# Two norms in a row computed from one residual, with the first one's rescale of the residual moved behind the next projection

## The chip, the cores and the metric

The kernel runs on one NeuronCore of a Trainium2 chip. Time is device time of one execution in microseconds. Five engines work from queues of their own: TensorE (PE) for matrix products, VectorE (DVE) and ScalarE (ACT) for elementwise work, GpSimd (POOL), which is idle around the change, and SyncE (SP), whose queue starts the loads of the weights.

## The reference

Two stacks of two layers each run over 256 tokens of 1024 features, in f32. The first stack ends with a norm of its own (`final_norm`), and the second one begins with a gated FFN that norms its input once more. What the change touches is this:

```python
RMS_EPS = EPS = 1e-6
def rms_norm(x, g):                       # _rms is the same
    x32 = x.astype(jnp.float32)
    y = x32 * lax.rsqrt(jnp.mean(x32 * x32, axis=-1, keepdims=True) + RMS_EPS)
    return (y * g.astype(jnp.float32)).astype(x.dtype)

def _swiglu(h, w_in, w_out):
    gate, up = jnp.split(h @ w_in, 2, axis=-1)
    return (jax.nn.silu(gate) * up) @ w_out

# end of the first stack
x = x + 0.5 * swiglu_ffn(rms_norm(x, ffn2_norm[1]), ffn2_w_in[1], ffn2_w_out[1])
x = rms_norm(x, final_norm)
# begin of the second one
x = x + 0.5 * _swiglu(_rms(x, norm_gain[0, 0]), ffn_w_in[0, 0], ffn_w_out[0, 0])
```

## The kernel before

The residual X lies in SBUF as eight chunks of 128 features by 256 tokens, so features are on the partitions. A product in f32 precision is made of three in the type fp32r: each operand is split into a high part (a copy rounded to fp32r, ScalarE) and a low part (what is left, VectorE), and TensorE adds high x high, low x high and high x low. The activations' parts are `Hh`/`Hl` (or `Ah`/`Al` inside an FFN), the weights' are `hi`/`lo`.

Weights come in slabs through a ring of four: SyncE loads a slab into `raw` (`sp_stage`), ScalarE makes `hi` (`act_hi`, L339), VectorE makes `lo` (`dve_lo`, L347), TensorE multiplies. A slab of the first projection of an FFN (`ffn_in`) has 8 weight tiles, so 24 products; one of the second projection (`ffn_out`) has 11, so 33, and two slabs make one tile of 128 output features. A load waits for the low part of the slab three places earlier; `act_hi` waits for TensorE to be done with the slab four places earlier.

An FFN with number n is the stages `ffn_in`n and `ffn_out`n. In `ffn_in` VectorE and ScalarE scale, gate and split each result (L724 `gate`, L701 Silu, L728 `up`, L732, L705 `Ah`, L736 `Al`). In `ffn_out` VectorE adds each tile to its chunk of X (`dve_resid`, L623), then chunk by chunk `prep` makes what the next norm and projection need: ScalarE makes `Hh`, the chunk times the next gain (L561), and its square (L565), VectorE makes `Hl` (L569) and adds the squares up in `SQSUM` (L576, L579). The factor 1/rms itself is a number per token and so is applied to the result of the projection (`R`, in L724 and L728), not to its input. So the next stage can start while the norm is still being computed: TensorE takes the first pair of slabs up to chunk 6 (`first_pair`, L451 to L453), then does the norm's sum over the partitions, one product of `SQSUM` with a matrix of ones (`norm`, L645), then chunk 7 of the pair, then the loop (L470, L475, L476). ScalarE takes the square root of the sum (L650) and VectorE the reciprocal (L655), which gives `R`.

The blocks run in this order: ffn0, rwkv (with the memory's keys), xattn0, ffn1, ffn2, gmlp, xattn1, ffn3, final, ffn4, hgrn, ffn5, ffn6, dil, ffn7. The block `final` is the class `FinalNorm`. It is set apart from the others by the list `UNSPLIT`: in `ffn_out3` `prep` makes only the squares. Then `FinalNorm` does the norm's product, 13 filler products that nothing reads (`pe_keep_awake`, L406), root and reciprocal, multiplies all eight chunks of X by gain and 1/rms (L1154), and makes `Hh`, `Hl` and the squares of the new X in one go. Each engine works its program in the order in which the blocks stand; there is no scheduler. ScalarE loads the table for the square root at the end of `act_resid` (L610) and that for Silu after the root (L652).

`ffn_out5` is a useful neighbour: there `prep` makes a second split of X for the attention's keys (`keys_hi`, L411, and `keys_lo`, L416), one operation more on each of the two engines in a tile.

## Time and profile before

| | us |
|---|---|
| median of three timed runs | 2582.8 |
| the three runs | 2577.11, 2582.8, 2590.47 |
| span of the profiled execution, first to last instruction | 2575.4 |
| TensorE busy in it | 2501.2 (97%) |
| VectorE busy | 1745.3 (68%) |
| ScalarE busy | 1318.1 (51%) |

The profiler took one execution of its own; its time beyond the span is not in the page. In the timeline views, a row gives the start, the busy time, engine, line, operation, written tile and read tiles, the count of instructions merged, and in brackets the idle time of the engine before it and what ended that. Products are pipelined: each has 0.28 us of its own, but they follow each other every 0.113 us at full clock. A product of full f32 type is two records.

### The profile page before, as it was taken

The page shows a single profiled execution, that of the slowest core. Times are in us where ns is not written, and L with a number is a line of the kernel's source. Part 1 is how long each engine was busy: PE and PEld are TensorE (multiplying, and loading weights), DVE is VectorE, ACT ScalarE, POOL GpSimd, SP SyncE. Part 2 cuts the span into 40 slices and gives each one's busy share as a digit, 9 for nine tenths or more (in the row PEclk, how much of TensorE's full clock was granted, in tenths as well). Part 3 has the DMA queues.
Part 4 walks back from the last instruction along what each step waited for, and adds up shares of the span by engine and source line. Part 5 has one row for each costly group of instructions (what it writes and reads, how often), then busy time and mean ns, then how long its engine had stood idle before and what let it go on. Part 6 is the DMA issues. An engine that isn't in the chain of part 4 may idle for free.

```text
span 2575.4 us, 60687 instructions
## 1 busy us (share of the span) xinstructions
PE 2501.2 (97%) x23366; PEld 2432.5 (94%) x23366; DVE 1745.3 (68%) x2868; ACT 1318.1 (51%) x1998; POOL 79.0 (3%) x122
## 2 busy tenths in 40 slices
PE   8998998999999999999999999899999999999999
PEld 7997877989999999989999999899999999999999
DVE  5757677567757667767757756967667666666774
ACT  5544544455545555545545547455555455555552
POOL 0000442000000000000000000000000000000000
PEclk9999999999999999999999999999999999999999
DMA  5663301435655655445654655235655665553564
GB/s 198 203 215 133 100 11 43 148 125 182 209 184 183 219 200 176 157 138 181 209 174 155 209 174 195 84 115 195 206 173 200 204 177 153 161 160 105 192 211 138
DMA packets 119681, 424.89 MB, mean 165 GB/s; under 512 B 16657, under 2 KB 24420, under 8 KB 119268
## 3 DMA queue, kind: packets, MB, share of 16 engines
q1 hardware_dynamic: 111328, 410.73, 47.6%
q10 hardware_dynamic: 8196, 11.96, 2.4%
q8 instruction: 112, 1.84, 0.3%
q14 instruction: 45, 0.37, 0.0%
HBM read 421.51 MB, written 1.12 MB: 164 GB/s over the span
## 4 chain that ended last, share of the span: by engine, by line
PE 89%; DVE 5%; ACT 3%; issue 2%; POOL 1%; DMA 0%; ACTq 0%; SPq 0%; DVEq 0%; POOLq 0%
PE bank L476 21%; PE bank L470 21%; PE bank L475 21%; PE bank L396 5%; PE bank L398 4%; PE bank L397 4%; PE bank L2327 1%; ACT hi L339 1%; PE bank L451 1%; PE bank L452 1%; PE bank L453 1%; DVE lo L347 1%; PE bank L1730 1%; PE bank L1703 1%; PE bank L1715 1%
## 5 line engine op out<-in xcount | busy, mean ns | idle before, releaser
L347 DVE TENSOR_TENSOR lo<-raw,hi 128x1024 fp32r<-128x1024 f32 (+1 forms) x728 | 935.0, 1292 | 380.6 <-ACT hi L339 378.8
L339 ACT ACTIVATE hi<-raw 128x1024 fp32r<-128x1024 f32 (+1 forms) x728 | 782.6, 1106 | 297.1 <-PE bank L398 170.6
L470 PE MATMUL bank<-Hh,hi 128*128 128x256 f32 x3056 | 845.5, 277 | 4.6 <-DVE lo L347 4.4
L476 PE MATMUL bank<-Hh,lo 128*128 128x256 f32 x3056 | 845.9, 277 | 0.0
L475 PE MATMUL bank<-Hl,hi 128*128 128x256 f32 x3042 | 840.8, 276 | 0.0
L470 PEld LDWEIGHTS bank<-Hh,hi 128*128 128x128 f32 x3056 | 574.5, 188 | 6.2 <-DVE lo L347 5.6
L476 PEld LDWEIGHTS bank<-Hh,lo 128*128 128x128 f32 x3056 | 574.5, 188 | 0.0
L475 PEld LDWEIGHTS bank<-Hl,hi 128*128 128x128 f32 x3042 | 572.2, 188 | 0.0
L476 PE MATMUL bank<-Ah,lo 128*128 128x256 f32 x1408 | 389.3, 277 | 0.0
L470 PE MATMUL bank<-Ah,hi 128*128 128x256 f32 x1408 | 388.6, 276 | 0.0
L475 PE MATMUL bank<-Al,hi 128*128 128x256 f32 x1400 | 386.4, 276 | 0.0
L470 PEld LDWEIGHTS bank<-Ah,hi 128*128 128x128 f32 x1408 | 264.3, 188 | 0.0
L476 PEld LDWEIGHTS bank<-Ah,lo 128*128 128x128 f32 x1408 | 264.3, 188 | 0.0
L475 PEld LDWEIGHTS bank<-Al,hi 128*128 128x128 f32 x1400 | 262.8, 188 | 0.0
L701 ACT ACTIVATE sgate<-gate 128x256 f32<-128x256 f32 x176 | 73.5, 418 | 232.2 <-DVE gate L724 232.2
L705 ACT ACTIVATE Ah<-act 128x256 f32 (+1 forms) x176 | 73.7, 419 | 209.1 <-DVE act L732 209.1
L623 DVE SCALAR_TENSOR_TENSOR X<-bank,X 128x256 f32<-128x256 f32 x112 | 47.4, 424 | 170.8 <-PE bank L476 163.1
L396 PE MATMUL bank<-Hh,hi 128*128 128x256 f32 x528 | 151.9, 288 | 0.0
L561 ACT ACTIVATE Hh<-X,vec 128x256 fp32r<-128x256 f32 x104 | 51.9, 503 | 193.6 <-DVE X L623 190.6
L398 PE MATMUL bank<-Hh,lo 128*128 128x256 f32 x528 | 147.7, 280 | 0.0
L397 PE MATMUL bank<-Hl,hi 128*128 128x256 f32 x528 | 147.7, 280 | 0.0
L396 PE MATMUL bank<-Kh,hi 128*128 128x256 f32 x384 | 112.3, 292 | 0.0
(429 smaller groups left out, 4038.8 us busy)
## 6 DMA issues: line engine op xcount, KB each, us to landing
raw<-in_w SPq DMA_DIRECT2D x600, 512.0 KB, 3.4
raw<-in_w SPq DMA_DIRECT2D x128, 704.0 KB, 4.5
dB<-dil_bias ACTq DMA_DIRECT2D x16, 384.0 KB, 10.4
X<-in_x SPq DMA_DIRECT2D x2, 512.0 KB, 5.3
mem_x<-in_mem ACTq DMA_DIRECT2D x2, 512.0 KB, 3.2
gWS<-in_ws ACTq DMA_DIRECT2D x1, 1024.0 KB
gBS<-in_bs ACTq DMA_DIRECT2D x1, 1024.0 KB
out_x<-X SPq DMA_DIRECT2D x4, 256.0 KB, 2.6
```

The costliest lines, as they stand in the source:

```text
L339: act.activation(k.hi[:, q, :w], k.raw[:, q, :w], ACT.Copy).then_inc(k.hi_ready, 1)
L347: dve.tensor_tensor(k.lo[:, q, :w], k.raw[:, q, :w], k.hi[:, q, :w].bitcast(F32), ALU.subtract).then_inc(k.lo_ready, 1)
L396: pe.matmul(out, wh, xh, start=first and kc == 0, stop=False)
L397: pe.matmul(out, wh, xl, start=False, stop=False)
L398: mm = pe.matmul(out, wl, xh, start=False, stop=last)
L470: pe.matmul(out, wh, xh, start=first, stop=False)
L475: pe.matmul(out, wh, xl, start=False, stop=False)
L476: mm = pe.matmul(out, wl, xh, start=False, stop=last)
L561: eng.activation(k.Hh[:, c, :], src[:, c, :], ACT.Copy, scale=k.v1(gain, c)).then_inc(k.h_hi, 1)
L623: dve.scalar_tensor_tensor(k.X[:, c, :], k.bank[s % RING][:, :T], coef, k.X[:, c, :], ALU.mult, ALU.add).then_inc(k.banks_freed, st.per_tile)
L701: act.activation(k.sgate[:, j, :], k.gate[:, j, :], ACT.Silu).then_inc(k.silu_done, 1)
L705: act.activation(k.Ah[:, bass.ds(m, 1), :].rearrange("p a t -> p (a t)"), k.act32[:, j, :], ACT.Copy).then_inc(k.ah_ready, 1)
```

## The change

With y = x r g, where r = 1/rms(x) and g is `final_norm`, the second norm is y r' g' with r' = 1/rms(y). Its mean of squares is r^2 mean((x g)^2), so r r' = 1/sqrt(mean((x g)^2) + eps mean(x^2) + eps^2). The changed kernel uses that:

- In `ffn_out3` `prep` splits the unscaled X times the product of both gains (`both_gains`, made once at the start of ffn3 on VectorE, 128x8), and adds up two sums: `SQSUM` of x^2 as before, and `FSUM` of (x g)^2 by way of `FSQ`. After the last chunk one fused operation adds eps times `SQSUM` to `FSUM`.
- ffn4 uses `norm_twice` in place of `norm`: two products on the matrix of ones into the halves of bank 4, two square roots (`STD` and `FSTD`), the load of the Silu table, and the reciprocal of the first, which is `R` for ffn4.
- `dve_final_norm` takes the reciprocal of `FSTD` and rescales X. It stands between ffn4's `ffn_in` and its first residual.
- The class `FinalNorm` with its fillers is gone.

```diff
@@ column_masks
-            low * HEAD ** -0.5, (1 - low) * HEAD ** -0.5]
+            low * HEAD ** -0.5, (1 - low) * HEAD ** -0.5, np.full(P, EPS * EPS)]
...
-UNSPLIT = ("final_norm", "mix_norm0")
+UNSPLIT = ("mix_norm0",)
...
@@ prep
-        k = self.k
+        k, twice = self.k, gain == "final_norm"
         ns, nq = self.split_n[e] + c, self.square_n[e] + c
+        scale = k.both_gains[:, c:c + 1] if twice else k.v1(gain, c)
         if e == "act":
...
+            if twice:
+                if c >= 2:
+                    eng.wait_ge(k.fsq_added, c - 1)
+                eng.activation(k.FSQ[:, c % 2, :], src[:, c, :], ACT.Square, scale=k.v1(gain, c)).then_inc(k.fsq_ready, 1)
         else:
...
+            if twice:
+                eng.wait_ge(k.fsq_ready, c + 1)
+                if c == 0:
+                    ins = eng.tensor_copy(k.FSUM[:], k.FSQ[:, 0, :])
+                else:
+                    eng.wait_ge(k.fsq_added, c)
+                    ins = eng.tensor_tensor(k.FSUM[:], k.FSUM[:], k.FSQ[:, c % 2, :], ALU.add)
+                ins.then_inc(k.fsq_added, 1)
+                if c == NC - 1:
+                    eng.wait_ge(k.fsq_added, NC)
+                    eng.wait_ge(k.sq_added, nq + 1)
+                    eng.scalar_tensor_tensor(k.FSUM[:], k.SQSUM[:], EPS, k.FSUM[:], ALU.mult, ALU.add).then_inc(k.fsum_ready, 1)
...
+    def norm_twice(self, eng, e, then=None):
+        k, n = self.k, self.norm_n[e]
+        if e == "pe":
+            self.square_n["pe"] += NC
+            eng.wait_ge(k.sq_added, self.square_n["pe"])
+            eng.wait_ge(k.fsum_ready, 1)
+            eng.matmul(k.bank[4][:, :T], k.ones, k.FSUM[:], start=True, stop=True)
+            eng.matmul(k.bank[4][:, T:], k.ones, k.SQSUM[:], start=True, stop=True).then_inc(k.ss_ready, 1)
+        elif e == "act":
+            eng.wait_ge(k.ss_ready, n + 1)
+            eng.wait_ge(k.rstd_ready, n)
+            eng.activation(k.STD[:], k.bank[4][:, :T], ACT.Sqrt, bias=k.col(C_EPS_SQUARED), scale=1.0 / D).then_inc(k.std_ready, 1)
+            eng.activation(k.FSTD[:], k.bank[4][:, T:], ACT.Sqrt, bias=k.col(C_EPS), scale=1.0 / D).then_inc(k.fstd_ready, 1)
+            eng.preload_act_table(then)
+        else:
+            eng.wait_ge(k.std_ready, n + 1)
+            eng.reciprocal(k.R[:], k.STD[:]).then_inc(k.rstd_ready, 1)
+        self.norm_n[e] += 1
+
+    def dve_final_norm(self, dve):
+        k = self.k
+        dve.wait_ge(k.fstd_ready, 1)
+        dve.reciprocal(k.FSTD[:], k.FSTD[:]).then_inc(k.frstd_ready, 1)
+        dve.wait_ge(k.frstd_ready, 1)
+        for c in range(NC):
+            dve.scalar_tensor_tensor(k.X[:, c, :], k.X[:, c, :], k.v1("final_norm", c), k.FSTD[:],
+                                     ALU.mult, ALU.mult).then_inc(k.x_scaled, 1)
+        dve.wait_ge(k.x_scaled, NC)
...
@@ FeedForward.dve
-        sh.norm(dve, "dve")
+        if self.next_gain == "final_norm":
+            g0, g1 = (k.vec[:, COL[n]:COL[n] + NC] for n in ("final_norm", GAIN_OF["ffn4"]))
+            dve.tensor_tensor(k.both_gains[:], g0, g1, ALU.mult).then_inc(k.both_ready, 1)
+        self.norm(dve, "dve")
...
         run(dve, st, body)
+        if self.normed_twice:
+            sh.dve_final_norm(dve)
         sh.dve_resid(dve, self.st_out, 0.5, self.next_gain, self.keys_next)
...
-class FinalNorm:
...
-    def pe(self, pe):
-        self.sh.norm(pe, "pe")
-        self.sh.pe_keep_awake(pe, 13, self.k.ones)
...
```

Where instructions stand, in the program's order. VectorE from the last residual chunk of `ffn_out3` on, before (L1154 is the rescale, L569 the low part of the activations):

```order
L623 SCALAR_TENSOR_TENSOR X<-bank,X 128x256
L579 TENSOR_TENSOR SQSUM<-SQSUM,SQ 128x256
L347 TENSOR_TENSOR lo<-raw,hi 128x1024 x2
L655 RECIPROCAL R<-STD 128x256
L1154 SCALAR_TENSOR_TENSOR X<-X,vec,R 128x256 x8
L569 SCALAR_TENSOR_TENSOR Hl<-X,vec,Hh 128x256
L576 COPY SQSUM<-SQ 128x256
L569 SCALAR_TENSOR_TENSOR Hl<-X,vec,Hh 128x256
L579 TENSOR_TENSOR SQSUM<-SQSUM,SQ 128x256
```

The same place in the changed program, from the last chunk's split on (L583 is the low part, L593 and L601 the two sums, L606 the fused one, L702 the reciprocal):

```order
L649 SCALAR_TENSOR_TENSOR X<-bank,X 128x256
L583 SCALAR_TENSOR_TENSOR Hl<-X,both_gains,Hh 128x256
L593 TENSOR_TENSOR SQSUM<-SQSUM,SQ 128x256
L601 TENSOR_TENSOR FSUM<-FSUM,FSQ 128x256
L606 SCALAR_TENSOR_TENSOR FSUM<-SQSUM,FSUM 128x256
L354 TENSOR_TENSOR lo<-raw,hi 128x1024 x2
L702 RECIPROCAL R<-STD 128x256
L206 UNCONDITIONAL_BRANCH
L206 ISA
L785 ISA
```

The reciprocal for ffn4 now stands right behind the weights' low parts. The rescale is not there any more; it stands behind the last low part of `ffn_in4` (L798), ahead of the first residual of `ffn_out4` (L649):

```order
L794 TENSOR_TENSOR act_59<-sgate,up 128x256
L354 TENSOR_TENSOR lo<-raw,hi 128x1408
L798 TENSOR_TENSOR Al<-act_59,Ah 128x256
L709 RECIPROCAL FSTD<-FSTD 128x256
L712 SCALAR_TENSOR_TENSOR X<-X,vec,FSTD 128x256 x8
L649 SCALAR_TENSOR_TENSOR X<-bank,X 128x256
L583 SCALAR_TENSOR_TENSOR Hl<-X,vec,Hh 128x256
```

TensorE from the last products of `ffn_out3` into the first pair of `ffn_in4`, before:

```order
L476 MATMUL bank<-Ah,lo 128x256
L518 REGISTER_ALU
L518 COMPARE_AND_BRANCH
L645 MATMUL bank<-SQSUM,masks 128x256
L406 MATMUL bank<-masks 128x256 x13
L451 MATMUL bank<-Hh,hi 128x256
L452 MATMUL bank<-Hl,hi 128x256
```

In the changed program the first pair follows the projection directly (L458 to L460), and the norm's products stand ahead of its chunk 7, two in a row:

```order
L460 MATMUL bank<-Hh,lo 128x256
L692 MATMUL bank<-FSUM,masks 128x256
L693 MATMUL bank<-SQSUM,masks 128x256
L458 MATMUL bank<-Hh,hi 128x256
L459 MATMUL bank<-Hl,hi 128x256
L460 MATMUL bank<-Hh,lo 128x256
```

So the norm's product, the 13 fillers and the second norm's product became two products inside the pair.

## Rows read from the trace of the kernel before

**Rows 1.** The page of the profile: its first line and part 1
```profile
span 2575.4 us, 60687 instructions
...
PE 2501.2 (97%) x23366; PEld 2432.5 (94%) x23366; DVE 1745.3 (68%) x2868; ACT 1318.1 (51%) x1998; POOL 79.0 (3%) x122
```

**Rows 2.** Timeline of TensorE at the final norm: start us, us, operation, count, [idle before]
```profile
1347.65 0.28 PE L476 MATMUL bank<-Ah,lo 128*128 128x256 f32 x1
1349.48 0.70 PE L645 MATMUL bank<-SQSUM,masks 128*128 128x256 f32 x2 [1.55 <-DVE SQSUM L579]
1350.02 5.78 PE L406 MATMUL bank<-masks 128*128 128x256 f32 x26
1358.33 0.55 PE L451 MATMUL bank<-Hh,hi 128*128 128x256 f32 x1 [2.54 <-DVE Hl L569]
...
1366.56 0.28 PE L470 MATMUL bank<-Hh,hi 128*128 128x256 f32 x1
```

**Rows 3.** Timeline of VectorE over the same stretch
```profile
1348.04 0.42 DVE L623 SCALAR_TENSOR_TENSOR X<-bank,X 128x256 f32<-128x256 f32 x1 [3.26 <-PE bank L476]
...
1352.62 1.75 DVE L655 RECIPROCAL R<-STD 128x256 f32<-128x256 f32 x1 [0.37 <-ACT STD L650]
1354.41 3.25 DVE L1154 SCALAR_TENSOR_TENSOR X<-X,vec,R 128x256 f32<-128x256 f32 x8
1357.70 0.48 DVE L569 SCALAR_TENSOR_TENSOR Hl<-X,vec,Hh 128x256 fp32r<-128x256 f32 x1
...
1362.69 0.48 DVE L569 SCALAR_TENSOR_TENSOR Hl<-X,vec,Hh 128x256 fp32r<-128x256 f32 x1
```

**Rows 4.** Stretches there: busy us (x) of PE, PEld, DVE, ACT, POOL; granted clock; DMA
```profile
1358.00:1360.00 2.00, 1.67 (x8) 1.70 (x9) 2.00 (x7) 1.58 (x5) 0.00 (x0) 0.54 0.00 0
1360.00:1362.00 2.00, 2.00 (x11) 1.91 (x11) 2.00 (x7) 2.00 (x6) 0.00 (x0) 0.60 0.00 0
```

**Rows 5.** Timeline of TensorE between the second and third FFN, with no norm between
```profile
771.84 0.28 PE L476 MATMUL bank<-Ah,lo 128*128 128x256 f32 x1
...
776.72 0.59 PE L645 MATMUL bank<-SQSUM,masks 128*128 128x256 f32 x2
776.96 0.47 PE L451 MATMUL bank<-Hh,hi 128*128 128x256 f32 x1
...
777.86 0.28 PE L470 MATMUL bank<-Hh,hi 128*128 128x256 f32 x1
```

**Rows 6.** Timeline of VectorE where the fourth FFN (ffn3) begins
```profile
1173.28 1.75 DVE L655 RECIPROCAL R<-STD 128x256 f32<-128x256 f32 x1 [2.11 <-ACT STD L650]
```

**Rows 7.** Timeline of VectorE in the projection ahead of the keys (ffn_out5)
```profile
1884.50 0.42 DVE L623 SCALAR_TENSOR_TENSOR X<-bank,X 128x256 f32<-128x256 f32 x1 [1.34 <-PE bank L476]
...
1891.98 0.42 DVE L623 SCALAR_TENSOR_TENSOR X<-bank,X 128x256 f32<-128x256 f32 x1 [2.46 <-PE bank L476]
...
1893.79 0.48 DVE L416 SCALAR_TENSOR_TENSOR Kl<-X,vec,Kh 128x256 fp32r<-128x256 f32 x1
```

**Rows 8.** Timeline of ScalarE between the second and third FFN
```profile
777.35 0.47 ACT L650 ACTIVATE STD<-bank,cols 128x256 f32<-128x256 f32 x1 [0.64 <-PE bank L645]
...
780.39 0.42 ACT L701 ACTIVATE sgate<-gate 128x256 f32<-128x256 f32 x1 [1.26 <-DVE gate L724]
```

**Rows 9.** Timeline of VectorE where ffn4's first projection ends and its second begins
```profile
1484.83 1.62 DVE L347 TENSOR_TENSOR lo<-raw,hi 128x1408 fp32r<-128x1408 f32 x1
1486.37 0.42 DVE L736 TENSOR_TENSOR Al<-act,Ah 128x256 fp32r<-128x256 f32 x1
1488.83 0.42 DVE L623 SCALAR_TENSOR_TENSOR X<-bank,X 128x256 f32<-128x256 f32 x1 [2.04 <-PE bank L476]
...
1491.40 3.16 DVE L347 TENSOR_TENSOR lo<-raw,hi 128x1408 fp32r<-128x1408 f32 x2 [0.81 <-ACT hi L339]
```

**Rows 10.** Timeline of TensorE in ffn4's second projection: first product, first on slab 4
```profile
1481.07 0.28 PE L470 MATMUL bank<-Ah,hi 128*128 128x256 f32 x1
...
1496.15 0.28 PE L470 MATMUL bank<-Ah,hi 128*128 128x256 f32 x1
```

More of the change, by code:

```diff
@@ L519, in pe_stage, with pe_first_stage @@
                 body(i)
-    def pe_first_stage(self, pe, st, late=False, pair=False):
+    def pe_first_stage(self, pe, st, late=False, pair=False, norm=None):
         self.split_n["pe"] += NC
-        self.pe_stage_h(pe, st, lambda: self.norm(pe, "pe"), late, pair=pair)
+        self.pe_stage_h(pe, st, lambda: (norm or self.norm)(pe, "pe"), late, pair=pair)
     def pe_stage_h(self, pe, st, after_first=None, late=False, rest=False, pair=False):
@@ L669, with __init__ @@
 class FeedForward:
-    def __init__(self, sh, name, order, nxt, keys_next=False, keys_now=False):
+    def __init__(self, sh, name, order, nxt, keys_next=False, keys_now=False, normed_twice=False):
         self.sh, self.k, self.n, self.next_gain = sh, sh.k, order, nxt
+        self.norm = sh.norm_twice if normed_twice else sh.norm
+        self.normed_twice = normed_twice
         self.keys_next, self.keys_now = keys_next, keys_now
@@ L681, in pe @@
             sh.pe_keep_awake(pe, 5, k.X[:, 0, :P], k.X[:, 1, :])
-        sh.pe_first_stage(pe, self.st_in, late=self.n == 0)
+        sh.pe_first_stage(pe, self.st_in, late=self.n == 0, norm=self.norm)
         done = 2 + FC * self.n
@@ L689, in act @@
         sh, k, st = self.sh, self.k, self.st_in
-        sh.norm(act, "act", ACT.Silu)
+        self.norm(act, "act", ACT.Silu)
         if self.keys_now:
@@ L1131, in dve @@
         sh.dve_resid(dve, self.so, 1.0, self.next_gain)
-class FinalNorm:
-    def __init__(self, sh, name, nxt):
-        self.sh, self.k, self.next_gain = sh, sh.k, nxt
-    def pe(self, pe):
-        self.sh.norm(pe, "pe")
-        self.sh.pe_keep_awake(pe, 13, self.k.ones)
-    def act(self, act):
-        k = self.k
-        self.sh.norm(act, "act")
-        self.sh.prep_all(act, "act", k.X, self.next_gain, wait=lambda c: act.wait_ge(k.x_scaled, c + 1))
-    def dve(self, dve):
-        k = self.k
-        self.sh.norm(dve, "dve")
-        dve.wait_ge(k.rstd_ready, self.sh.norm_n["dve"])
-        for c in range(NC):
-            dve.scalar_tensor_tensor(k.X[:, c, :], k.X[:, c, :], k.v1("final_norm", c), k.R[:],
-                                     ALU.mult, ALU.mult).then_inc(k.x_scaled, 1)
-        dve.wait_ge(k.x_scaled, NC)
-        self.sh.prep_all(dve, "dve", k.X, self.next_gain)
 class Hgrn2:
@@ L3004, in make_blocks @@
         gain = "final_norm" if nxt == "final" else GAIN_OF.get(nxt)
+        if b == "final":
+            continue
         if b.startswith("ffn"):
-            out.append(FeedForward(sh, b, n_ffn, gain, keys_next=b == "ffn5", keys_now=b == "ffn6"))
+            out.append(FeedForward(sh, b, n_ffn, gain, keys_next=b == "ffn5", keys_now=b == "ffn6",
+                                   normed_twice=n > 0 and flow[n - 1] == "final"))
             n_ffn += 1
@@ L3010, in make_blocks @@
     return out
-MIXERS = {"rwkv": Rwkv7, "xattn": CrossAttention, "gmlp": GatedMlp, "final": FinalNorm, "hgrn": Hgrn2, "dil": Dilated}
+MIXERS = {"rwkv": Rwkv7, "xattn": CrossAttention, "gmlp": GatedMlp, "hgrn": Hgrn2, "dil": Dilated}
 def program(nc, io, blocks, counts):
```

15 lines of the change are left out of this document (12 added, 3 removed).

## The prediction

> **What bounds the kernel now.** I read the page first, then the timeline of each engine around the place of the change. The page says that TensorE is busy for 97% of the span [rows 1]. So a saving counts only where TensorE stands still, or where it does work that the result doesn't need. The view to read is therefore TensorE's timeline around the final norm [rows 2]: the last product of the second FFN projection before it starts at 1347.65, the norm's sum of squares follows at 1349.48, then 13 filler products on the ones mask (26 records) from 1350.02 to 1355.80, then nothing until 1358.33, when the first pair of weight slabs of the next FFN begins. The ordinary loop of that stage starts at 1366.56. From the last product to that loop is 1366.56 - 1347.65 = 18.91 us.
>
> Who holds it up there is in VectorE's timeline [rows 3]. The last residual chunk is written at 1348.04. Then comes the reciprocal (1352.62, 1.75 us), the rescale of all eight chunks of X (1354.41, 3.25 us), and only then the split of the rescaled X into its low part: first at 1357.70, last at 1362.69, one each 0.71 us. TensorE can't start the pair before 1358.18, when the first low part is there. It also starts with the granted clock at 0.54 and 0.60 of full speed [rows 4], at the lower of its two levels (1.2 GHz) for most of those 4 us, after it had stood still for 2.5 us. The half clock cost little in this execution, since the low parts came each 0.71 us and three products take 3 x 0.213 = 0.64 us at that level (estimate: 256 columns at 1.2 GHz).
>
> What the same stretch costs without a norm in between is in the same trace: between two FFNs of the first stack [rows 5] the last product starts at 771.84, the norm's sum at 776.72, the loop at 777.86. That is 6.02 us, in which TensorE never stands still: it does the 42 products on chunks 0 to 6 while the eighth chunk is being prepared.
>
> **The change, part by part.** Sum of the boundary, if the changed one runs like [rows 5]: 18.91 - 6.02 = **12.89 us saved**. It holds the reciprocal, the rescale, the eight splits, the fillers and the half clock together, so none of them is to be counted a second time. The first pair needs low parts of chunks 0 to 6, which now come along with the projection before it, two slabs and two free banks, which the program has ready in the same order as in [rows 5].
>
> *One more product.* The norm now has two products of full f32 type on the ones mask, where it had one. The 13 fillers took 5.78 us at full clock, so 5.78 / 13 = 0.445 us each [rows 2]. The lower bound is the 0.24 us from the start of such a product to that of the next one behind it (776.72 to 776.96 [rows 5]); that row leaves out what the products behind it lose (the first of them has 0.47 instead of 0.28 us). I take 0.44, since the fillers stand back to back, as these two do: **0.44 us lost**. Here 12.89 - 0.44 = 12.45.
>
> *The product of the two gains*, 128x8 on VectorE at the start of the FFN before: VectorE is idle for 2.11 us there, waiting for the square root [rows 6], and an operation 32 times as large takes 0.42. Nothing.
>
> *More work in each of the eight tiles of the projection before.* ScalarE gets the high part and a second square, VectorE the low part and a second add. The projection ahead of the keys has exactly one operation more on each engine than an ordinary split one, and so the same count [rows 7]: its tiles follow each other at 1891.98 - 1884.50 = 7.48 us, which is TensorE's 66 products, and VectorE still waits 1.34 us in a tile for TensorE. So nothing; if the cover were gone it would cost what goes beyond 1.34, eight times.
>
> *The wait of the norm on the second sum.* TensorE's norm products now wait for a fused operation that adds eps times the first sum to the second. TensorE comes to them 4.88 us after the last product (776.72 - 771.84 [rows 5]), at 1347.65 + 4.88 = 1352.53. The sum is ready earlier: the residual is at 1348.04; in the keys' projection the second extra operation starts 1.81 us behind the residual (1891.98 to 1893.79 [rows 7]), so the last add ends near 1350.3; I allow 0.3 for waits and 0.48 for the fused one: 1351.1. It is early by 1.4 us. Queued behind it on VectorE are the low parts of slabs 2 and 3; the first of them takes no longer than the 1.62 us of a wider one [rows 9], so it is ready by 1352.7, and TensorE wants it at 1347.65 + 6.02 + 0.44 = 1354.1.
>
> *A second square root* on ScalarE, between the first and the load of the Silu table: 0.47 us at most. ScalarE waits 1.26 us ahead of the first Silu [rows 8]. Nothing. Both norms' sums have to be there before the first root starts, but that delay is the 0.44 us already counted, and VectorE's reciprocal moves by as much as TensorE.
>
> *The rescale moved behind the first projection of the next FFN.* This is the one place where a margin gets thin. VectorE's last low part of that projection ends at 1486.79 now [rows 9]. Behind it go the reciprocal and the rescale: 1.79 us (1352.62 to 1354.41) and 3.29 us (1354.41 to 1357.70) [rows 3]. They end at 1491.87. The residual of the first tile, which now starts at 1488.83, is 3.04 us late. It frees no bank that is wanted soon. But ScalarE's split of slabs 4 and 5 is queued behind the operations that wait for this residual, and VectorE's low part of slab 4 starts 2.57 us behind it (1488.83 to 1491.40) and takes 1.62 us [rows 9]: 1491.87 + 2.57 + 1.62 = 1496.06. TensorE takes up slab 4 at 1496.15 [rows 10]. So **0 us, with 0.1 us to spare**. The next tile starts with VectorE 1.2 us late and its slab 6 has 1.8 us to spare. Weight loads on SP's queue for slabs 8 and 9 wait for the same low parts and go out 3 us later, for splits 7 us away. The bounds: -0 us, and 0.6 us lost if the eight operations don't overlap (8 x 0.476 = 3.81, not 3.25) and the two waits cost a little.
>
> The Trainium skill, "VectorE: DVE Perf Modes", section "The DRAIN you can't avoid", says that after each VectorE operation the next doesn't start until the pipe is empty. Taken strictly, the eight rescales would last 3.81 us and TensorE would wait about 0.5 us here; the row shows eight of 0.476 us in 3.25 us, so they do overlap, and I go by the row.
>
> Sum: 12.89 - 0.44 - 0 = **12.45 us**. The profiled execution has a span of 2575.4 us [rows 1] and should come to 2563.0. The page gives no time of that execution beyond the span; the three timed runs lie 1.7 to 15.1 us above it, and their median of 2582.8 by 7.4 us. The change touches nothing outside the span, so I take the same difference off the median: **2582.8 - 12.45 = 2570.3 us**, 0.48% less.
>
> **The rivals.**
>
> *A: the boundary before is dearer in ordinary runs than in the profiled one.* The half clock fell here on the products that waited for VectorE anyway [rows 3, 4]. Falling on the others, it costs up to 0.1 us for each of some 15 products, 1.5 us. The chip decides this anew in each execution. For it: the stretch with less clock lies by chance. Against: it begins after a rest, and the rest has its place. It gives 2582.8 - 13.9 = 2568.9.
>
> *B: the moved rescale stalls TensorE after all.* For it: 0.1 us of margin made from five rows. If VectorE comes out of the loop up to 1 us later than now, as ScalarE's second root may bring about, TensorE waits 1 us once, and the tiles behind catch up (2 x 1.34 us to spare). 2571.3; with two such waits 2572.
>
> *C: the wait only moves.* The first pair would start at once but stand at the norm for the second sum. That needs the sum 1.4 us later than I have it, for example if each of the added operations of the last tile took double. Up to 2 us then, 2572 to 2573.
>
> *D: slower than before.* The added operations make ScalarE and VectorE the bound of the projection before. The room is 1.34 us in a tile as [rows 7] show it, with as many operations on each engine as the changed one has. To eat 12.45 us it would take 1.34 + 12.45 / 8 = 2.9 us in each tile beyond what the keys' projection has, from which point the kernel is slower. What is added in a tile is two operations on each engine, each like the low part's 0.48 us [rows 3], and [rows 7] hold both. For 3.5 us in a tile: 2582.8 - 12.45 + 8 x 2.16 = 2587.6. Nothing in the rows speaks for it.
>
> The Trainium skill, "TensorE: Matmul & The Clock Gate", section "Part 1: The HAM clock gate", says that the lower clock is the default and that only activity lifts it. The trace agrees where it shows it: 0.54 and 0.60 granted behind the pause, full clock in the boundary without one.
>
> **How the numbers follow.** The forecast of 12.45 us gets 0.78, A 0.08, B 0.09, C 0.03, D 0.02. The predicted time is the forecast's. About 0.5% is what a measurement of this kernel can tell from no change, and 0.5% of 2582.8 is 12.9 us, 0.45 us more than I forecast. The three runs before are 13.4 us apart, so their median, and that of the changed kernel, is good to some 5 us. The forecast thus falls on both sides of the line: of its 0.78 I give 0.38 to faster by over 0.5%, 0.39 to within, 0.01 to slower. A gives 0.06 and 0.02, B 0.03 and 0.06, C 0 and 0.02 with 0.01 slower, D 0.01 within and 0.01 slower. Together 0.47, 0.50, 0.03. The range: down to 2570.3 - 1.5 (A) - 0.2 (a second product at 0.24) - 5 = 2563.6, up to 2570.3 + 1.7 (B or C) + 5 = 2577.0; rounded, 2563 to 2577.
>
> **What the profile after will show.** From the last product of the projection before to the first of the loop: 6.46 us, with no idle time and full clock. Two norm products, 0.44 us apart. The rescale of X at about 1474 to 1479 (the times above less 12.45) on VectorE between the last low part and the first residual; the first residual 3 us later against TensorE than now. The first product on slab 4 of that projection 15.1 us behind its first one; more than 15.2 makes it B. A wait of TensorE's norm on VectorE makes it C. Tiles of the projection before of 7.48 us; more makes it D. A span that is shorter by 12.5 with other times shorter by much more or less would mean that the rest of the kernel doesn't run alike in both, which nothing here lets me foresee.

## The result and the profile after

| us | before | after |
|---|---|---|
| median | 2586.6 (4 runs, 2577.1 to 2590.7) | 2664.5 (4 runs, 2661.3 to 2665.0) |
| the profiled execution, and its span | span 2575.4 | 2661.3, span 2659.5 |

The changed kernel takes 1.0315 times as long, with a 95% interval of 1.029 to 1.034. I had forecast 2570.3, in a range of 2563 to 2577: it is 94 us above the forecast and outside the range, on the side to which I gave a chance of 0.03.

The page after, which answers to [rows 1]. The lines of its part 5 give count, busy us and mean ns of one:

```profile
span 2659.5 us, 60644 instructions
...
PE 2595.2 (98%) x23340; PEld 2530.0 (95%) x23340; DVE 1760.2 (66%) x2870; ACT 1327.8 (50%) x1998; POOL 79.1 (3%) x122
...
PE 93%; DVE 3%; ACT 2%; issue 1%; POOL 1%; DMA 0%; ACTq 0%; SPq 0%; DVEq 0%; POOLq 0%
...
L477 PE MATMUL bank<-Hh,hi 128*128 128x256 f32 x3056 | 865.6, 283 | 4.0 <-DVE lo L354 3.9
...
L477 PEld LDWEIGHTS bank<-Hh,hi 128*128 128x128 f32 x3056 | 586.7, 192 | 5.2 <-DVE lo L354 5.2
```

The same two groups of before (there the lines are L470):

```profile
L470 PE MATMUL bank<-Hh,hi 128*128 128x256 f32 x3056 | 845.5, 277 | 4.6 <-DVE lo L347 4.4
...
L470 PEld LDWEIGHTS bank<-Hh,hi 128*128 128x128 f32 x3056 | 574.5, 188 | 6.2 <-DVE lo L347 5.6
```

TensorE has 26 records less and 94 us more of busy time. No new wait appears: the idle time ahead of the loop's first product in a slab is even a little smaller (4.0 us against 4.6), and TensorE makes up 93% of the chain of work that ended last. The same 3056 products simply take longer, 283 ns against 277, and their weight loads 192 ns against 188.

How far they lie apart is seen where TensorE never stops. TensorE's timeline in `ffn_in3`, which the change doesn't touch, first before, then after:

```profile
1210.28 0.28 PE L470 MATMUL bank<-Hh,hi 128*128 128x256 f32 x1
1210.39 0.28 PE L475 MATMUL bank<-Hl,hi 128*128 128x256 f32 x1
1210.51 0.28 PE L476 MATMUL bank<-Hh,lo 128*128 128x256 f32 x1
1210.62 0.28 PE L470 MATMUL bank<-Hh,hi 128*128 128x256 f32 x1
```

```profile
1209.98 0.28 PE L458 MATMUL bank<-Hh,hi 128*128 128x256 f32 x1
1210.10 0.28 PE L459 MATMUL bank<-Hl,hi 128*128 128x256 f32 x1
1210.22 0.28 PE L460 MATMUL bank<-Hh,lo 128*128 128x256 f32 x1
1210.34 0.28 PE L458 MATMUL bank<-Hh,hi 128*128 128x256 f32 x1
```

(L458 to L460 are the first pair of slabs, which the slower kernel is still at.) Three products take 0.34 us before and 0.36 after. Over 100 us it can be counted. The view of stretches gives busy us (and instructions) of PE, PEld, DVE, ACT and POOL, then the granted clock (1.00 is full), DMA share and GB/s; first before, then after:

```profile
1200.00:1300.00 100.00, 100.00 (x885) 100.00 (x884) 70.72 (x109) 51.38 (x72) 0.00 (x0) 1.00 0.61 205
```

```profile
1200.00:1300.00 100.00, 100.00 (x834) 99.94 (x833) 69.97 (x111) 52.25 (x75) 0.00 (x0) 1.00 0.55 180
```

885 products against 834, so one each 113.0 ns (100 us / 885) against 119.9 ns, both at full granted clock. I call this the pace. (The view also counts the two or three products that only reach into the stretch, so a pace from it is 0.1 to 0.4 ns too short. From start to start, over the same 100 us of the two traces, it is 113.3 and 120.0 ns.) The other engines do their work at the old speed (108 to 112 operations for 70 us on VectorE), and DMA moves less because less is asked for. The slower pace holds from the beginning of the kernel to its end. The kernel has 18,624 such products (600 slabs of 24, 128 of 33); 6.7 ns on each would be 125 us. The span grew by less, 84.1 us, or some 96 with the saving at the boundary, since some stages wait for other engines and some ran at a middle pace before as well (below).

And yet the boundary, for which the change was made, went as forecast. TensorE's timeline there after, which answers to [rows 2]:

```profile
1396.96 0.28 PE L483 MATMUL bank<-Ah,lo 128*128 128x256 f32 x1
...
1402.12 0.59 PE L692 MATMUL bank<-FSUM,masks 128*128 128x256 f32 x2
1402.55 0.59 PE L693 MATMUL bank<-SQSUM,masks 128*128 128x256 f32 x2
...
1403.69 0.28 PE L477 MATMUL bank<-Hh,hi 128*128 128x256 f32 x1
```

6.73 us from the last product to the loop, with no idle time, against 18.91 before. So the question is what the change does to products that it doesn't contain.

### The profile page after: what moved, and what is told of

The parts are those of the page before. It is cut to its first block, busy times and chain, and to the rows that moved or that the text cites. A ratio compares the mean times of both kernels' runs of the same rounds, so it can differ in the third digit from the quotient of the medians.

```text
span 2659.5 us, 60644 instructions
## 1 busy us (share of the span) xinstructions
PE 2595.2 (98%) x23340; PEld 2530.0 (95%) x23340; DVE 1760.2 (66%) x2870; ACT 1327.8 (50%) x1998; POOL 79.1 (3%) x122
## 4 chain that ended last, share of the span: by engine, by line
PE 93%; DVE 3%; ACT 2%; issue 1%; POOL 1%; DMA 0%; ACTq 0%; SPq 0%; DVEq 0%; POOLq 0%
PE bank L483 22%; PE bank L477 22%; PE bank L482 22%; PE bank L403 5%; PE bank L404 5%; PE bank L405 5%; PE bank L2365 1%; PE bank L458 1%; PE bank L459 1%; PE bank L460 1%; PE bank L1768 1%; ACT hi L346 1%; PE bank L1741 1%; PE bank L1753 1%; PE bank L917 1%
## 5 line engine op out<-in xcount | busy, mean ns | idle before, releaser
L346 ACT ACTIVATE hi<-raw 128x1024 fp32r<-128x1024 f32 (+1 forms) x728 | 792.3, 1107 | 409.6 <-PE bank L483 207.3
L477 PE MATMUL bank<-Hh,hi 128*128 128x256 f32 x3056 | 865.6, 283 | 4.0 <-DVE lo L354 3.9
L483 PE MATMUL bank<-Hh,lo 128*128 128x256 f32 x3056 | 866.3, 283 | 0.0
L482 PE MATMUL bank<-Hl,hi 128*128 128x256 f32 x3042 | 861.1, 283 | 0.0
L477 PEld LDWEIGHTS bank<-Hh,hi 128*128 128x128 f32 x3056 | 586.7, 192 | 5.2 <-DVE lo L354 5.2
L483 PEld LDWEIGHTS bank<-Hh,lo 128*128 128x128 f32 x3056 | 586.7, 192 | 0.0
L482 PEld LDWEIGHTS bank<-Hl,hi 128*128 128x128 f32 x3042 | 584.0, 192 | 0.0
L483 PE MATMUL bank<-Ah,lo 128*128 128x256 f32 x1408 | 399.3, 284 | 0.0
L477 PE MATMUL bank<-Ah,hi 128*128 128x256 f32 x1408 | 398.6, 283 | 0.0
L482 PE MATMUL bank<-Al,hi 128*128 128x256 f32 x1400 | 396.3, 283 | 0.0
L477 PEld LDWEIGHTS bank<-Ah,hi 128*128 128x128 f32 x1408 | 270.3, 192 | 0.0
L649 DVE SCALAR_TENSOR_TENSOR X<-bank,X 128x256 f32<-128x256 f32 x112 | 47.4, 423 | 204.6 <-PE bank L483 196.1
L403 PE MATMUL bank<-Hh,hi 128*128 128x256 f32 x528 | 153.7, 291 | 0.0
L404 PE MATMUL bank<-Hl,hi 128*128 128x256 f32 x528 | 149.6, 283 | 0.0
L405 PE MATMUL bank<-Hh,lo 128*128 128x256 f32 x528 | 149.5, 283 | 0.0
```

Source lines behind the costliest of these rows:

```text
L346: act.activation(k.hi[:, q, :w], k.raw[:, q, :w], ACT.Copy).then_inc(k.hi_ready, 1)
L403: pe.matmul(out, wh, xh, start=first and kc == 0, stop=False)
L404: pe.matmul(out, wh, xl, start=False, stop=False)
L405: mm = pe.matmul(out, wl, xh, start=False, stop=last)
L477: pe.matmul(out, wh, xh, start=first, stop=False)
L482: pe.matmul(out, wh, xl, start=False, stop=False)
```

## The experiments

**What the change does to memory.** In the order in which the program reserves SBUF, bytes per partition, come `raw`, `hi`, `lo` (the weights' ring), small tables with `cols` among them, then the arena, which starts at the next multiple of 64 and holds all activations at fixed places. The change adds `both_gains` (32 bytes) and one column to `cols` (which grows from 96 to 100 bytes and is rounded up by 32). Either of them pushes the arena on by 64:

```
              hi      lo     arena   distance arena - hi, modulo 256
before     39040   61568    106816   192
after      39040   61568    106880     0
```

(The distance to `lo` is the same, since `lo` - `hi` = 22528 = 88 x 256; and every part of `Hh`, `Hl`, `Ah`, `Al` that a product reads lies a multiple of 256 behind the start of the arena.) These addresses come from how the program reserves memory, not from the trace. The first theory was: **the pace depends on where the activations lie**. Its rival: **it depends on the program's instructions or data** that the change brings, and the addresses are innocent.

### Before, with 32 unused bytes; after, with 64 unused bytes

```diff
         self.sel = sb("sel", [P, NC * 16])
+        self.pad = sb("pad", [P, 8])
```

> The kernel before with one unused tensor of 32 bytes per partition allocated ahead of the arena, which is the size of both_gains; nothing reads or writes it. All activation tiles start 64 bytes later, as in the changed kernel (arena at 106880, a multiple of 128, in place of 106816, 64 past one); the weights' ring stays. Theory 1, the address decides: the fp32r products follow each other every 0.1197 us instead of 0.1133, and the time is that of the changed kernel plus the 12.45 us of boundary, 2674 to 2680 us. Rival 2, the program decides (the order of instructions, the missing pause): no change, 2577 to 2591 us.

Measured: 2677.4 us (4 runs), 1.0354 (1.034 to 1.037). Its stretch, to be read beside the two above:

```profile
1200.00:1300.00 100.00, 100.00 (x835) 99.95 (x834) 71.17 (x112) 53.67 (x78) 0.00 (x0) 1.00 0.55 179
```

A tensor that nothing reads or writes costs the kernel of before 94 us. The rival has fallen. With the same arena the changed kernel is faster than this one by 2677.4 - 2664.5 = 12.9 us, close to the 12.45 that the change was forecast to bring.

The other direction, `self.pad = sb("pad", [P, 16])` behind `both_gains` in the changed kernel (arena 106944):

> The changed kernel with an unused tensor of 64 bytes per partition ahead of the arena, so that the arena starts at 106944, again 64 past a multiple of 128. Theory 1 with 128 bytes as the period: products every 0.1133 us again, 2568 to 2578 us, 12 us under the kernel before. Rival 2, the program decides: unchanged 2661 to 2665 us. If the period is longer than 128 bytes, something between.

Measured: 2624.5 us (6 runs), 1.0163 (1.0146 to 1.018), 852 products in the stretch, 117.4 ns. The theory of a period of 128 fell. A third pace exists.

### The change with the addresses of before

`both_gains` gets a free place inside the arena, and eps^2 is kept as one more vector in `vec`, whose size rounds up to the same:

```diff
-    + [("v_norm", 2 * D), ("a_out_gain", P), ("k_gain", 3 * P), ("q_gain", 3 * P)]
+    + [("v_norm", 2 * D), ("a_out_gain", P), ("k_gain", 3 * P), ("q_gain", 3 * P), ("eps_squared", P)]
...
-            low * HEAD ** -0.5, (1 - low) * HEAD ** -0.5, np.full(P, EPS * EPS)]
+            low * HEAD ** -0.5, (1 - low) * HEAD ** -0.5]
...
-        self.both_gains = sb("both_gains", [P, NC])
...
+        self.both_gains = self.at("both_gains", 90 * KB, [P, NC])
...
-            eng.activation(k.STD[:], k.bank[4][:, :T], ACT.Sqrt, bias=k.col(C_EPS_SQUARED), scale=1.0 / D).then_inc(k.std_ready, 1)
+            eng.activation(k.STD[:], k.bank[4][:, :T], ACT.Sqrt, bias=k.v1("eps_squared", 0), scale=1.0 / D).then_inc(k.std_ready, 1)
```

> The changed kernel with the addresses of the kernel before: both_gains lies inside the arena and eps squared in a spare column of vec, so every tile that both kernels have lies where it lay. Theory 1: 12.45 us under the kernel before, ratio 0.9952, about 2570 to 2575 us, with the boundary of 6.46 us. Rival 2: 2661 to 2665 us, since the order of the work is that of the changed kernel.

Measured: **2570.5 us** (7 runs, 2565.5 to 2578.8) beside 2583.7 of before (10 runs, 2575.3 to 2588.1), ratio 0.9954 (0.9939 to 0.9969). The same instructions on the same data, 94 us faster than the changed kernel, and faster than the kernel before.

```profile
span 2563.7 us, 60644 instructions
```

```profile
1200.00:1300.00 100.00, 100.00 (x885) 100.00 (x884) 70.61 (x110) 51.95 (x74) 0.00 (x0) 1.00 0.62 205
```

This is the version to use, and the one on which the steps of the prediction can be judged.

### Before with 128 unused bytes

As the first, with `[P, 32]` (arena 106944).

> The kernel before with an unused tensor of 128 bytes per partition ahead of the arena, which moves the activations by 128 bytes to 106944, 64 past a multiple of 128 but another multiple of it. Theory 1 with a period of 128 bytes: unchanged, 2577 to 2591 us. With a longer period: slower, up to 2680 us. Rival 2: unchanged.

Measured: 2635.3 us (4 runs), 1.0196 (1.0179 to 1.0213), 851 products. It agrees with the changed kernel at the same arena, 10.8 us above it. The reading with a period of 128 is out for good.

### Own address, or distance?

All that follows is built on the version with the addresses of before. The next two separate "the arena has a bad address" from "arena and ring lie badly to each other". One moves ring and arena together, the arena to 106880, where the changed kernel has it:

```diff
+        self.pad = sb("pad", [P, 16])
         self.raw = sb("raw", [P, RING, WIDE * P])
```

> An unused tensor of 64 bytes ahead of the ring, so ring and activations both move by 64 bytes; the activations start at 106880 like in the changed kernel, but their distance from the ring is that of the kernel before. Theory R: 113 ns, 2570 us. Theory A: 120 ns, 2662 us.

Measured: 2570.6 us (8 runs), 0.9967 (0.9946 to 0.9988). The other leaves the arena at 106816 and moves the ring by 1216 (`vec` and `cols` reserved ahead of `raw`), so that the distance is 0:

> The tensors vec and cols are allocated ahead of the ring in place of behind it, so the ring moves up by 1216 bytes (192 modulo 256) and the activations stay at 106816. Their distance from the ring becomes 0 modulo 256. Theory R: 120 ns, 2662 us, as in the changed kernel. Theory A: 113 ns, 2570 us.

Measured: 2662.5 us (2 runs), 1.0309 (1.0272 to 1.0345). The stretches of these two:

```profile
1200.00:1300.00 100.00, 100.00 (x884) 100.00 (x884) 70.47 (x108) 51.64 (x73) 0.00 (x0) 1.00 0.62 203
```

```profile
1200.00:1300.00 100.00, 100.00 (x835) 99.94 (x834) 69.97 (x111) 52.26 (x75) 0.00 (x0) 1.00 0.55 180
```

Fast at the "bad" address, slow at the "good" one. Of the two, it is the **distance** that counts. X and some of the small tables moved with the ring in these runs; the part on what else touches SBUF comes back to them.

### Other distances

With a pad of `[P, 48]` behind `sel` (arena + 192) and with one of `[P, 8]` and the arena's base rounded to 32 (arena + 32):

> The changed kernel with the addresses of the kernel before, and an unused tensor that moves the activations by 192 bytes to 107008, 128 bytes (modulo 256) from the weights' ring. So far the distance from the ring (modulo 256) gave 113 ns per product at -64, 120 at 0, 117.5 at +64. Theory R, the distance between the two operands decides: 128 is farthest from 0, so 113 ns or less, 2570 us or less. Theory A, the activations' own address decides (64, 128, 192 modulo 256 gave 113, 120, 117.5): at 0 nothing is known, and by the trend from 192 up to 256 the time lies at 2570 to 2625 us.

> The same with activations moved by 32 bytes only, to 106848, 32 bytes below the ring's alignment. Theory R: between the values at -64 and at 0, some 115 to 118 ns and 2600 to 2640 us, if the overlap grows step by step; 113 or 120 if it is all or nothing. Theory A says the same. It is to show the shape.

Measured: 2639.7 and 2635.2 us (2 runs each), 1.022 (1.0184 to 1.0256) and 1.0203 (1.0168 to 1.0237). These are the distances 128 and 224. For 128 both theories missed (2570 us or less, and 2570 to 2625). Distance 128, the farthest from 0, is no better than its neighbours: a rule by which what is farthest from 0 is fastest is out.

Three more distances, by `cols` ahead of `raw` (96), the same with a pad of 64 (160), and `vec` and `cols` ahead of `raw` with a pad of 32 (32); one run each, so without an interval:

> The changed kernel with both_gains in the arena; the tensor cols lies ahead of the ring, which puts the activations 96 bytes (modulo 256) from the weights. Measured so far: 0 gives 120.0 ns per product, 64 gives 117.5, 128 gives 118.5, 192 gives 113.6, 224 gives 118.2. Theory R (the distance decides, modulo 256): a value between 113 and 120, near those of 64 and 128, 117 to 119 ns, 2620 to 2645 us. Theory R64 (only the distance modulo 64 and a little more decide): as 224, 118.2 ns, 2635 us.

> The same with a distance of 160 bytes. Theory R: between the 118.5 ns at 128 and the 113.6 at 192. If 192 is the middle of a gap between two readers, 160 is like 224, 118 ns and 2635 us; if the gap lies between 128 and 192, it is the fastest of all, under 113 ns and under 2565 us.

> The same with a distance of 32 bytes (vec and cols ahead of the ring, the arena 32 bytes later). Theory R: between the 120.0 ns at 0 and the 117.5 at 64, 2640 to 2660 us.

Measured: 2664.7, 2628.5 and 2612.4 us. The first and the third missed. All distances together, the pace from the number of products in 1200 to 1300 us:

| distance mod 256 | products in 100 us | ns each | us |
|---|---|---|---|
| 0 (three kernels) | 834, 835, 835 | 119.8 to 119.9 | 2664.5, 2677.4, 2662.5 |
| 32 | 852 | 117.4 | 2612.4 |
| 64 (two kernels) | 852, 851 | 117.4, 117.5 | 2624.5, 2635.3 |
| 96 | 835 | 119.8 | 2664.7 |
| 128 | 843 | 118.6 | 2639.7 |
| 160 | 855 | 117.0 | 2628.5 |
| **192** (three kernels) | 885, 885, 884 | 113.0, 113.1 | 2586.6, 2570.5, 2570.6 |
| 224 | 845 | 118.3 | 2635.2 |

(2677.4, 2635.3 and 2586.6 are without the change, and so some 12 us higher.) Kernels with equal distance agree, but there is no simple law in it. (By the starts, the 113.0 of the table is 113.3, the 117.4 is 117.8 and the 119.8 is 120.0.) Of eight distances only that of the kernel before is fast in this stage; the kernels with the change at the others take 1.6% to 3.7% longer than the 2570.5 us (2612.4 / 2570.5 and 2664.7 / 2570.5).

### One of the two weight tensors alone

A pad of 64 bytes between `hi` and `lo` puts `hi` at distance 0 and leaves `lo` at 192; `vec` and `cols` between them do the opposite.

> The changed kernel at the addresses of the kernel before, with 64 unused bytes between the weights' high and low parts: hi has the distance 0 from the activations (slow), lo has 192 (fast). While one product streams its activations, the weights of the next one are loaded. Theory L, these two reads get in each other's way: only the product during which lo is loaded, Hl x hi, is followed at once (113.6 ns from it to Hh x lo), the other two steps take 120 ns; mean 117.9, 2630 us. Theory S, a product's own weights against its own activations: the step behind Hh x lo is the short one. If it is neither, all three steps are alike.

> The changed kernel with vec and cols allocated between the weights' high and low parts: hi is 192 bytes (modulo 256) from the activations (fast), lo 0 (slow). If each weight load pays for its own distance, one load in three is slow: mean (2 x 113.6 + 120) / 3 = 115.7 ns, 2600 us. If lo alone decides, 120 ns and 2662 us; if hi alone decides, 113.6 ns and 2570 us (but then the mirror would have been at 120, and it was at 117.7).

Measured: 2623.0 and 2626.0 us (one run each), and these stretches:

```profile
1200.00:1300.00 100.00, 100.00 (x851) 100.00 (x851) 71.76 (x112) 51.31 (x74) 0.00 (x0) 1.00 0.58 191
```

```profile
1200.00:1300.00 100.00, 100.00 (x852) 100.00 (x850) 71.24 (x112) 51.83 (x75) 0.00 (x0) 1.00 0.57 189
```

If each product paid for the place of its own weights, the first would have two slow steps and one fast in three, the second one slow and two fast: (2 x 120.0 + 113.3) / 3 = 117.8 and (120.0 + 2 x 113.3) / 3 = 115.5 ns. From start to start both have 117.8, so the second decides against it. The single steps, from the starts in the same 100 us, are 117.4, 117.6 and 118.3 ns in the first, and 117.6, 118.3 and 117.4 in the second (high x high, low x high, high x low, each to the next product). No step is short in either, so it isn't a price for each product by its own weights. Theory L had the first run's sum nearly right (117.9 ns and 2630 us) by luck: the one short step from which it got it isn't there. One badly placed tensor slows the stream as a whole, to a pace between the two.

### The kernel before, profiled again

A long stage of the version with the addresses of before (`ffn_in6`) ran at another pace than before, at one and the same distance. To see how much of that belongs to a kernel and how much to an execution, the kernel before was run once more, unchanged.

> The kernel before, unchanged, profiled a second time. In its first profile nearly all long stages ran at 113.4 ns per product, and mem_kv (958 to 998 us, gmlp's first projection's end) at 118. Theory V (settled anew in each execution): other stages at 118, and the span differs from 2575.4 by some 5 us for each long stage that changed. Theory P (fixed by the program): the same stages, and the span within 2 us of it but for pauses of the clock.

Measured: 2574.2 us, span 2572.4. It is mixed. One short stretch differs between the two executions of one program, first the first profile, then the second:

```profile
1625.00:1635.00 10.00, 10.00 (x91) 10.00 (x90) 8.99 (x12) 6.03 (x6) 0.00 (x0) 1.00 0.51 175
```

```profile
1625.00:1635.00 10.00, 10.00 (x87) 10.00 (x86) 9.13 (x12) 6.03 (x6) 0.00 (x0) 1.00 0.52 164
```

while `gmlp` at 967 to 992 us has 215 and 214 products in 25 us, 116.3 and 116.8 ns, in both, and the long `ffn_in6` is at 113 ns in both executions of the kernel before but at 117.4 in the version with the same addresses, and in the one with ring and arena both moved by 64. The rows of these two, and that of the kernel before:

```profile
1900.00:2000.00 100.00, 100.00 (x852) 100.00 (x851) 71.06 (x112) 51.35 (x74) 0.00 (x0) 1.00 0.60 197
1900.00:2000.00 100.00, 100.00 (x852) 100.00 (x851) 69.73 (x110) 52.04 (x74) 0.00 (x0) 1.00 0.60 199
```

```profile
1920.00:2020.00 100.00, 100.00 (x885) 100.00 (x884) 71.58 (x110) 50.91 (x73) 0.00 (x0) 1.00 0.62 209
```

So even at the good distance a stage can fall into the middle pace, and it then stays there to its end. One long stage at 117.4 instead of 113.0 costs some 4 us in each 100. As far as these profiles show, for `ffn_in6` this goes with the kernel and not with the execution: both executions of the kernel before have `ffn_in6` fast, both kernels with the change at this distance have it slow (the second of them also has a slow stretch from about 1470 to 1540 us, which costs it 2 us). Between the two executions of the kernel before only short stretches differ. So no profile here shows the 13 us by which the runs of one kernel differ to come from the pace of its long stages; where they come from stays open.

**What else touches SBUF.** Loads into the ring and the splits on ScalarE and VectorE read and write SBUF too, and could collide with TensorE's reads. But the pace doesn't need them. In the last microseconds of the kernel nothing is left to load or to split; the changed kernel first, then the version with the addresses of before:

```profile
2647.00:2654.00 7.00, 7.00 (x60) 7.00 (x60) 0.00 (x0) 0.00 (x0) 0.00 (x0) 1.00 0.00 0
```

```profile
2551.60:2558.30 6.70, 6.70 (x61) 6.69 (x60) 0.00 (x0) 0.00 (x0) 0.00 (x0) 1.00 0.00 0
```

No other engine and no DMA is at work, and TensorE's products read only `hi`, `lo`, `Ah` and `Al`. Still they start every 120.0 ns in the first and every 113.3 in the second (56 steps in each), as in the long stages. In the changed kernel with 64 unused bytes the same place has 117.8. So neither X nor the tables that moved with the ring are needed for it, nor the loads, nor the splits. The one way left for them would be that they set a pace earlier that then holds on.

**What stays open.** That the distance between ring and activations sets the pace is shown, in both directions and with unused bytes alone. What in the chip makes it is not. TensorE reads both operands from SBUF at once, the moving one for the running product and the weights for the next (a weight load is in the trace for 188 to 192 ns, longer than the step to the next product), and a collision of these two streams would fit a dependence on their distance, its spreading over all three steps, and paces that lock in. They are also the only SBUF traffic in the two stretches above. But no run looked at the memory itself, and nothing here says why 192 is fast and 96 is as slow as 0, or why a long stage at 192 takes the middle pace.

## Why the prediction failed

**The step that failed** is one line of the part-by-part section: "*The product of the two gains*, 128x8 on VectorE ... Nothing." It costed the operation and not its tensor. The 32 bytes of that tensor, and the column of eps^2, which had no term at all, move all activations by 64 bytes, and that costs 2659.5 - 2563.7 = 95.8 us of span. What carried this into the forecast is the sum itself, "12.89 - 0.44 - 0 = **12.45 us**", from which "should come to 2563.0" follows: it holds the boundary alone, so I took for granted that whatever isn't edited runs alike. What the runs show in its place is a cost in work that nobody edited: where the operands lie 0 in place of 192 bytes apart (modulo 256), the slab products start every 120.0 ns in place of 113.3, from the beginning of the kernel to its end. The last part did name the sign ("A span that is shorter by 12.5 with other times ... would mean that the rest of the kernel doesn't run alike in both"), but no case in the sum stood for it. [rows 1] should have warned me: at 97% TensorE, everything that changes its pace by 1% is worth 25 us, twice the whole change. That the arena moves could be worked out from the two new reservations. That it costs something, and which way, could not be read from one trace, so the honest course would have been a rival with a wide price.

**The Trainium skill**, "TensorE: Matmul & The Clock Gate", section "Part 2: What happens when you issue a matmul", says that TensorE has two independent read ports into SBUF, so that loading the next weights takes no read bandwidth from the running product. The measurement differs: the same product starts every 113.3 or every 120.0 ns by nothing but the distance of the two operands, with no other engine and no DMA at work. Its section "Part 1: The HAM clock gate (the "warmup" mystery)" gives columns / 2.4 GHz and some 2.5 ns from one product to the next, by estimate 109.2 ns for 256 columns. None of the streams above, in which every product has a weight load of its own, reached that: the best is at 113.3, some 4 ns above it.

**The boundary was right.** All steps are judged in the version with the addresses of before. TensorE there:

```profile
1347.10 0.28 PE L483 MATMUL bank<-Ah,lo 128*128 128x256 f32 x1
...
1351.97 0.59 PE L692 MATMUL bank<-FSUM,masks 128*128 128x256 f32 x2
1352.40 0.59 PE L693 MATMUL bank<-SQSUM,masks 128*128 128x256 f32 x2
...
1353.54 0.28 PE L477 MATMUL bank<-Hh,hi 128*128 128x256 f32 x1
```

From last product to loop 6.44 us (forecast 6.46), the norm 4.87 us behind the last product (4.88), the two norm products 0.43 us apart (0.44).

**Rival C, the norm waits for the second sum:** no. VectorE at that place:

```profile
1347.49 0.42 DVE L649 SCALAR_TENSOR_TENSOR X<-bank,X 128x256 f32<-128x256 f32 x1 [2.46 <-PE bank L483]
...
1349.87 0.43 DVE L606 SCALAR_TENSOR_TENSOR FSUM<-SQSUM,FSUM 128x256 f32<-128x256 f32 x1
1350.21 2.35 DVE L354 TENSOR_TENSOR lo<-raw,hi 128x1024 fp32r<-128x1024 f32 x2
```

The sum is ready at 1350.30, 2.81 us behind the last residual (I had 3.1), and TensorE wants it at 1351.97: early by 1.7 us. I had 1.4.

**The second root:** ScalarE's rows:

```profile
1353.03 0.47 ACT L697 ACTIVATE STD<-bank,vec 128x256 f32<-128x256 f32 x1 [0.67 <-PE bank L693]
1353.41 0.47 ACT L698 ACTIVATE FSTD<-bank,cols 128x256 f32<-128x256 f32 x1
...
1356.08 0.42 ACT L760 ACTIVATE sgate<-gate 128x256 f32<-128x256 f32 x1 [0.90 <-DVE gate L786]
```

The idle time ahead of the first Silu is 0.90 us, from 1.26 [rows 8]: 0.36 us of it eaten, none lost.

**Rival D, the tile before becomes the bound:** no. In VectorE's timeline the tiles of `ffn_out3` follow each other at 7.48 us, with 1.33 us of idle time, where [rows 7] had 1.34:

```profile
1332.53 0.42 DVE L649 SCALAR_TENSOR_TENSOR X<-bank,X 128x256 f32<-128x256 f32 x1 [1.33 <-PE bank L483]
...
1340.01 0.42 DVE L649 SCALAR_TENSOR_TENSOR X<-bank,X 128x256 f32<-128x256 f32 x1 [1.33 <-PE bank L483]
```

In the changed kernel as it was given they lie 7.92 us apart, and VectorE waits longer for TensorE, not shorter:

```profile
1381.51 0.42 DVE L649 SCALAR_TENSOR_TENSOR X<-bank,X 128x256 f32<-128x256 f32 x1 [1.78 <-PE bank L483]
...
1389.43 0.42 DVE L649 SCALAR_TENSOR_TENSOR X<-bank,X 128x256 f32<-128x256 f32 x1 [1.78 <-PE bank L483]
```

The 0.44 us more are 66 products at 6.7 ns. My sign for D ("more makes it D") would have been misread here: a longer tile shows only that something is slower, and the idle time beside it tells which.

**Rival B, the moved rescale stalls TensorE:** just touched. VectorE, and behind it TensorE's first product of the stage and the first on slab 4:

```profile
1473.40 0.42 DVE L798 TENSOR_TENSOR Al<-act,Ah 128x256 fp32r<-128x256 f32 x1
1473.74 1.75 DVE L709 RECIPROCAL FSTD<-FSTD 128x256 f32<-128x256 f32 x1
1475.52 3.26 DVE L712 SCALAR_TENSOR_TENSOR X<-X,vec,FSTD 128x256 f32<-128x256 f32 x8
1478.88 0.43 DVE L649 SCALAR_TENSOR_TENSOR X<-bank,X 128x256 f32<-128x256 f32 x1
...
1481.46 3.16 DVE L354 TENSOR_TENSOR lo<-raw,hi 128x1408 fp32r<-128x1408 f32 x2 [0.80 <-ACT hi L346]
```

```profile
1468.05 0.28 PE L477 MATMUL bank<-Ah,hi 128*128 128x256 f32 x1
...
1483.14 0.38 PE L477 MATMUL bank<-Ah,hi 128*128 128x256 f32 x1
1483.36 0.28 PE L482 MATMUL bank<-Al,hi 128*128 128x256 f32 x1
```

The waits view of this stretch has one line for TensorE:

```profile
PE bank L477 <- DVE lo L354: 0.2, 1, 0.2
```

The residual comes 10.83 us behind the stage's first product, where I had 1491.87 - 1481.07 = 10.80; slab 4 is taken up at 15.09 (I had 15.08). The 0.1 us of margin was as thin as that, and it fell on the other side: the product on slab 4 takes 0.38 us, and the next one follows 0.22 us behind it instead of 0.11. The price is 0.1 us.

**The sum.** Forecast 12.45 us. Measured at the distance of before: 13.2 us by the medians, and 11.9 by the ratio (8.0 to 15.8). At distance 0 the change is worth 12.9 us (2677.4 - 2664.5), at 64 it is worth 10.8 (2635.3 - 2624.5), and with ring and arena both moved by 64, which is the distance of before again, 9.5 (2580.1 - 2570.6). The whole time thus confirms the 12.45 only to some us. The traces do it closely. The loop's high x high products (L470 before, L477 now) are 4848 in both, and can be compared start by start in the profiles: the changed version is 0.56 us ahead up to the boundary and 13.02 ahead behind it, so the boundary gave **12.46 us**. Behind slab 4 of `ffn_out4` it is 12.89 ahead. In the slow `ffn_in6` it loses another 4.7 us (13.25 to 8.52), and it gains 3.2 back between 2067 and 2410 us of the kernel before, where the second execution of the kernel before gains 3.0 on the first with no change at all. That is how 11.7 us of span (2575.4 - 2563.7) come about. With ring and arena both moved by 64 the boundary gives 12.46 too. By the medians and intervals alone, rival A can't be told from the forecast by runs that differ by 13 us among themselves.

## What to carry to other kernels

A kernel whose TensorE is busy for 97% of the time, as this one's, can be sensitive to where its operands lie: before and after every edit compare the addresses of weights and activations, and when an edit shifts them, put the new small tensors into a free place or behind everything else. If the time moves by more than the edit can explain, count the products in 100 us of a stage that wasn't edited; if that number has changed at full granted clock, the cause isn't the work that the edit adds or takes away, and where it put things comes first on the list. A pad of unused bytes is then the cheapest experiment, and trying the eight steps of 32 bytes may be worth more than the next clever change.

## What was unexpected of the hardware

- The distance of weights and moving operand modulo 256 bytes sets the pace of 256-column products in three parts of fp32r: by the counts in 1200 to 1300 us, 113.0 ns at 192, 117.0 to 118.6 at 32, 64, 128, 160 and 224, 119.8 to 119.9 at 0 and 96. That 256 is the period is an assumption: only one kernel tests it, that with the ring moved by 1216, whose distance is 66,560 where the changed kernel's is 67,840, with the same remainder and the same pace. Multiples of 512 don't matter in any of the kernels: weight tiles lie 512 bytes apart and chunks of activations 1024, so the distance changes by such steps from product to product, and the pace stays.
- The loads, the splits and the other engines aren't needed for it: with none of them at work for 7 us it is 120.0 and 113.3 ns from start to start, as elsewhere.
- With one of two weight tensors at 0 and the other at 192, the products run at 117.4 to 117.5 ns by the counts, and no one of the three steps is short. At distance 32 the three steps are unlike (119.2, 115.8 and 118.3 ns from start to start), with the same mean of 117.8.
- At distance 192 the long `ffn_in6` runs at 113.0 ns in the kernel before and at 117.4 with the change, and a short stretch changes between two executions of one program (91 and 87 products in 10 us).
- TensorE shows as busy for 100% in all of these paces. Only the count and the mean of one (277 or 283 ns; weight loads 188 or 192 ns) tell them apart.
